# A two-block transformer kernel: norms at four stage borders done by token halves

## The reference, cut to what matters

```python
def _rms(t, g):
    y = t * lax.rsqrt(jnp.mean(t * t, axis=-1, keepdims=True) + NORM_EPS)
    return y * g
def _modulate(t, g, shift, scale):
    return _rms(t, g) * (1 + scale) + shift
def _swiglu(h, w13, w2):
    gte, up = jnp.split(h @ w13, 2, axis=-1)
    return (jax.nn.silu(gte) * up) @ w2
...
lat = lat + 0.5 * mod[:, 0, 2] * _swiglu(_modulate(lat, norm_g[i, 0], mod[:, 0, 0], mod[:, 0, 1]), ffn_w13[i, 0], ffn_w2[i, 0])
h = _modulate(lat, norm_g[i, 1], mod[:, 1, 0], mod[:, 1, 1])
...
lat = lat + mod[:, 1, 2] * y
```

## Time and profile before

| | |
|---|---|
| median of three runs | 2087.09 us |
| profiled execution | 2086.57 us, span 2084.8 us |
| mean granted TensorE clock | 0.961 |
| PE busy | 1910.5 us (92%) |
| DVE busy | 1403.1 us (67%) |
| ACT busy | 683.8 us (33%) |
| POOL busy | 123.0 us (6%) |
| DMA | 315.79 MB, 151 GB/s over the span |

### The profile page before, as it was taken

How to read it: one execution, slowest core, us unless ns; L and a number is a source line. 1 busy time by engine, 2 the same in 40 slices (tenths; PEclk the granted TensorE clock), 3 DMA queues, 4 the chain that set the end, 5 groups by cost and what they waited for, 6 DMA issues and landing times.

```text
span 2084.8 us, 26715 instructions
## 1 busy us (share of the span) xinstructions
PE 1910.5 (92%) x10092; PEld 1624.6 (78%) x10092; DVE 1403.1 (67%) x2091; ACT 683.8 (33%) x910; POOL 123.0 (6%) x78
## 2 busy tenths in 40 slices
PE   2975799799999998997999999989999998889998
PEld 2954788678888887886888888878888887679998
DVE  7868899876666666668766666776665225856554
ACT  2443356332222223332322222132222123444432
POOL 2000200200000110002000001100000010010000
PEclk9976899899999999998999999999999999999999
DMA  9840955433334443434244334424433323223444
GB/s 377 309 176 26 247 193 198 156 120 141 133 148 148 154 172 121 151 131 159 113 151 149 133 140 168 167 110 151 151 138 115 101 93 120 91 81 141 164 162 158
DMA packets 75738, 315.79 MB, mean 151 GB/s; under 512 B 19060, under 2 KB 22904, under 8 KB 56344
## 3 DMA queue, kind: packets, MB, share of 16 engines
q1 hardware_dynamic: 75136, 314.15, 42.6%
q10 hardware_dynamic: 536, 0.79, 0.1%
HBM read 313.86 MB, written 1.06 MB: 151 GB/s over the span
## 4 chain that ended last, share of the span: by engine, by line
PE 74%; DVE 17%; ACT 3%; issue 2%; DMA 1%; SPq 1%; POOL 0%; DVEq 0%; ACTq 0%
PE acc L1296 72%; DVE Wl L811 4%; ACT Wh L526 2%; DVE tmp L798 2%; PE psN L1296 1%; DVE psGT L843 1%; DVE psGT L846 1%; DVE najunk L846 1%; DVE najunk L843 1%; DMA afirst<-in_ada_w 1%; DVE small L968 1%; DVE XT L798 1%; DVE psGT L840 1%; DVE tmp L986 1%; PE psN L1358 0%
## 5 line engine op out<-in xcount | busy, mean ns | idle before, releaser
L1296 PE MATMUL acc<-Hh,Wh 128*128 128x512 f32 (+1 forms) x2320 | 808.4, 348 | 50.1 <-DVE Hl L798 24.2
L1296 PE MATMUL acc<-Hl,Wh 128*128 128x512 f32 (+1 forms) x2320 | 800.3, 345 | 0.0
L1296 PE MATMUL acc<-Hh,Wl 128*128 128x512 f32 (+1 forms) x2320 | 799.6, 345 | 0.0
L811 DVE TENSOR_TENSOR Wl<-raw,Wh 128x2048 fp32r<-128x2048 f32 (+1 forms) x214 | 449.6, 2101 | 273.4 <-ACT Wh L526 273.3
L1296 PEld LDWEIGHTS acc<-Hh,Wh 128*128 128x128 f32 x2320 | 448.3, 193 | 113.7 <-issue 46.0
L526 ACT ACTIVATE Wh<-raw 128x2048 fp32r<-128x2048 f32 (+1 forms) x214 | 374.3, 1749 | 350.0 <-PE acc L1296 331.8
L1296 PEld LDWEIGHTS acc<-Hl,Wh 128*128 128x128 f32 x2320 | 448.6, 193 | 50.7 <-issue 0.7
L1296 PEld LDWEIGHTS acc<-Hh,Wl 128*128 128x128 f32 x2320 | 447.9, 193 | 50.4
L1296 PE MATMUL acc<-hidh,Wh 128*128 128x512 f32 (+1 forms) x704 | 258.6, 367 | 0.9 <-DVE Wl L811 0.9
L1296 PE MATMUL acc<-hidl,Wh 128*128 128x512 f32 (+1 forms) x704 | 258.3, 367 | 0.0
L1296 PE MATMUL acc<-hidh,Wl 128*128 128x512 f32 (+1 forms) x704 | 258.2, 367 | 0.0
(11 more groups left out here) (222 smaller groups left out, 1189.9 us busy)
## 6 DMA issues: line engine op xcount, KB each, us to landing
raw<-in_ffn_up SPq DMA_DIRECT2D x88, 1024.0 KB, 4.8
graw<-in_mod_w SPq DMA_DIRECT2D x144, 512.0 KB, 5.5
raw<-in_ffn_down SPq DMA_DIRECT2D x64, 704.0 KB, 4.1
graw<-in_ada_w SPq DMA_DIRECT2D x32, 512.0 KB, 6.8
raw<-in_odd_in SPq DMA_DIRECT2D x16, 1024.0 KB, 5.0
raw<-in_even_in SPq DMA_DIRECT2D x12, 1024.0 KB, 7.2
raw<-in_conv_in SPq DMA_DIRECT2D x12, 1024.0 KB, 4.8
afirst<-in_ada_w SPq DMA_DIRECT2D x8, 1024.0 KB, 13.1
```

Source lines behind the costliest of these rows:

```text
L811: nc.vector.tensor_tensor(Wl[:, half, 0:f], raw[:, slot, 0:f], Wh[:, half, 0:f].bitcast(f32), ALU.subtract)\
L1296: return nc.tensor.matmul(out, lhsT, rhs, start=start, stop=stop)
```

## The change

At the four borders into conv_in, ffn1_up, ffn2_up and gqa_kv (`HALVED`) the last tiles, the norm and the first two tiles are done by halves of the tokens. The latent half is CL, the context half CC.

- The last output (the last two down tiles, or the last tile of conv_out) is made for the latent columns first, then for the context columns. The latent residual, squares, sums, mean, root and spread go on beside the context columns of PE. New semaphores `lat_*` order them.
- `halves_norm` on DVE runs the eight latent chunks and then the eight context chunks. The context residual stands behind the third latent chunk, the context mean behind the sixth.
- The split of the first weight tile moves from before the last down tile to between the first latent chunks, in two halves of 1024 columns; the second tile's split is also halved and stands behind the sixth and the eighth latent chunk. (At ffn1_up the first tile is split whole behind the latent mean.)
- On PE the first two tiles run as: tile 0 latent, tile 1 latent, tile 0 context, tile 1 context. In gqa_kv: keys latent, value blocks 0 and 1, keys context, value blocks 2 and 3.
- conv_out makes one modulation row a tile instead of two (its four tiles), gqa_out one instead of none.

The core of the diff:

```diff
-    ("conv_out", 4, 16, 0, TOK, 2, "dve"),
+    ("conv_out", 4, 16, 0, TOK, 1, "dve"),
...
-    ("gqa_out", 4, 16, 0, LAT, 0, "dve"),
+    ("gqa_out", 4, 16, 0, LAT, 1, "dve"),
...
+            def halves_norm(name, meanwhile):
...
+                dve.wait_ge(lat_done, l + 1)
+                residual_half(0, CL).then_inc(lat_res, 1)
+                meanwhile()
+                mean(0, psN, lat_ss, l + 1).then_inc(lat_mean, 1)
+                if not ffn:
+                    split(S[name].n0)
+                dve.wait_ge(lat_spread, l + 1)
+                scaled(0, 0, CL, psN).then_inc(lat_t, 1)
+                for k in range(KC):
+                    if k + 1 < KC:
+                        if k > 0:
+                            dve.wait_ge(lat_ready, KC * l + k)
+                        scaled(k + 1, 0, CL, psN).then_inc(lat_t, 1)
+                    if ffn and k < 2:
+                        split_half(S[name].n0, k)
+                    dve.wait_ge(lat_hi, KC * l + k + 1)
+                    low(k, 0, CL).then_inc(lat_ready, 1)
+                    if k in (5, 7):
+                        split_half(S[name].n0 + 1, k // 2 - 2)
+                    if k == 2:
+                        dve.wait_ge(tile_done, s.n0 + s.tiles)
+                        residual_half(1, CC).then_inc(drained["dve"], 1)
+                    if k == 5:
+                        mean(1, psT[1], n_ss, i + 1).then_inc(n_mean, 1)
...
+                def last_halved():
...
+                    part(0, 0, CL)
+                    sum_of_sums(name)
+                    part(0, 1, CL).then_inc(lat_done, 1)
+                    part(1, 0, CC, lat_sums).then_inc(tile_done, 1)
+                    lat_spreads(name)
+                    part(1, 1, CC).then_inc(tile_done, 1)
...
+                pe.wait_ge(lo_ready, s.n0 + 1)
+                part(0, CL, lat_ready, KC * l, {3: ctx_sums, 7: ctx_spread})
+                pe.wait_ge(lo_ready, s.n0 + 2)
+                pe.wait_ge(drained["dve"], prev.drained1)
+                part(1, CL, lat_ready, KC * l, {})
+                part(0, CC, h_ready, H0[name], {}).then_inc(tile_done, 1)
+                part(1, CC, h_ready, H0[name], {}).then_inc(tile_done, 1)
...
+                if name in HALVED:
+                    n0, ffn = S[name].n0, S[X_FROM[name]].tiles > KC
+                    if ffn:
+                        split_half(n0, 0)
+                    for k in range(KC):
+                        if k == 1 and ffn:
+                            split_half(n0, 1)
+                        if k in (4, 6):
+                            split_half(n0 + 1, k // 2 - 2)
+                        act.wait_ge(lat_t, KC * HALVED[name] + k + 1)
+                        nc.scalar.activation(Hh[:, k, CL], tmp[:, k % 2, CL], ACT.Identity, bias=affine(name, k, 0)[1])\
+                            .then_inc(lat_hi, 1)
+                        if k == 2:
+                            act.wait_ge(drained["dve"], S[X_FROM[name]].drained1)
+                            for q in LAST[name]:
+                                square_half(name, q, CC)
```

More of the change, by code:

```diff
@@ L212, in build @@
         c_tanh = sem("c_tanh")
+        hi_half = sem("hi_half")
+        lat_done, lat_res, lat_sq, lat_ss, lat_mean, lat_rstd, lat_spread, lat_t, lat_hi, lat_ready = (
+            sem("lat_" + x) for x in ("done", "res", "sq", "ss", "mean", "rstd", "spread", "t", "hi", "ready"))
         nmx = small[:, 0:64]
@@ L292, in build, with halved @@
         X_TO = {f: n for n, f in X_FROM.items()}
+        HALVED = {n: i for i, n in enumerate(["conv_in", "ffn1_up", "ffn2_up", "gqa_kv"])}
+        LAST = {n: (KC - 2, KC - 1) if n == "ffn1_up" else (KC - 1,) for n in HALVED}
+        LAT_SQ0 = {n: sum(len(LAST[m]) for m in HALVED if HALVED[m] < HALVED[n]) for n in HALVED}
+        CL, CC = slice(0, LAT), slice(LAT, TOK)
+        def halved(s):
+            return X_TO.get(s.name) in HALVED
         def summed_of(s):
@@ L1304, in three, with first_two_halved, part @@
                 return mm(out, wl, xh, False, last)
+            def first_two_halved(s):
+                name, prev = s.name, S[X_FROM[s.name]]
+                l = HALVED[name]
+                def part(t, c, ready, base, beside):
+                    n = s.n0 + t
+                    for k in range(KC):
+                        pe.wait_ge(ready, base + k + 1)
+                        for j in range(2):
+                            last = three(acc[t][j][:, c], n % SPLIT, j * KC + k, Hh[:, k, c], Hl[:, k, c], k == 0, k == KC - 1)
+                        if k in beside:
+                            beside[k](name)
+                    return last
+                pe.wait_ge(lo_ready, s.n0 + 1)
[5 more added lines that the diff above has]
+                part(1, CC, h_ready, H0[name], {}).then_inc(tile_done, 1)
@@ new lines, in lat_sums, with lat_spreads @@
+            def lat_sums(name):
+                pe.wait_ge(lat_sq, LAT_SQ0[name] + len(LAST[name]))
+                for q in LAST[name]:
+                    for b in range(2):
+                        ins = nc.tensor.matmul(psN[:, b:b + 1], tmp[:, q % 2, b * P:(b + 1) * P], ones[:, 0:1],
+                                               start=False, stop=q == KC - 1, skip_group_check=True)
+                ins.then_inc(lat_ss, 1)
+            def lat_spreads(name):
+                pe.wait_ge(lat_rstd, HALVED[name] + 1)
+                for b in range(2):
+                    ins = spread(psN[:, b * P:(b + 1) * P], rstd, b)
+                ins.then_inc(lat_spread, 1)
@@ new lines, in ctx_sums, with ctx_spread @@
+            def ctx_sums(name):
+                pe.wait_ge(n_sq, KC * NORMS[name] + KC)
+                for q in LAST[name]:
+                    for b in range(2):
+                        ins = nc.tensor.matmul(psT[1][:, b:b + 1], tmp[:, q % 2, (2 + b) * P:(3 + b) * P], ones[:, 0:1],
+                                               start=False, stop=q == KC - 1, skip_group_check=True)
+                ins.then_inc(n_ss, 1)
+            def ctx_spread(name):
+                pe.wait_ge(n_rstd, NORMS[name] + 1)
+                for b in range(2):
+                    ins = spread(psT[1][:, b * P:(b + 1) * P], rstd, 2 + b)
+                ins.then_inc(n_spread, 1)
@@ L1322, in step @@
                     last.then_inc(tile_done, 1)
-                if begin:
+                if begin or halved(s):
                     for t in range(begin, s.tiles):
                         step(t, t % SPLIT, t // SPLIT)
+                elif s.name in HALVED:
+                    first_two_halved(s)
+                    tiles(pe, s, SPLIT, 0, lambda t, u, i: None if isinstance(t, int) and t < SPLIT else step(t, u, i), head=1)
                 else:
@@ L1363, in sum_of_sums @@
                 pe.wait_ge(n_sum, SUM0[name] + SUMMED[name])
+                if name in HALVED:
+                    for h, bank in enumerate((psN, psT[1])):
+                        for b in range(2):
+                            nc.tensor.matmul(bank[:, b:b + 1], tmp[:, 2, (2 * h + b) * P:(2 * h + b + 1) * P], ones[:, 0:1],
+                                             start=b == 0, stop=False, skip_group_check=True)
+                    return
                 sum_of(name, tmp[:, 2, :], True, False)
```

126 lines of the change are left out of this document (116 added, 10 removed).

## The result

The changed kernel took 2077.81 us (median of 5, 2076.37 to 2078.04) against 2087.49 for the kernel before (2086.03 to 2087.95): ratio 0.995, 95% interval 0.9939 to 0.9961. That is 9.7 us less; 13.3 were forecast, and the time is inside the range. The profiled execution took 2077.92, its span is 8.7 shorter. The page of after, beside the earlier trace rows: the span, the engines' busy time, and the shares of the chain of waits.

The account below looks back on a forecast made before the run. PE, busy 92%, was taken as the bound, with time to win only at stage borders. 4.6 + 5.8 + 3.3 + 4.9 - 3.7 = 14.9, less 1.6 for hand-overs, left 13.3: 2073.8 us, range 2067 to 2083.

Parts of the forecast that it names:

- conv_in, 4.6: Border into conv_in: last pair's start to second tile's end falls from 49.5 to 44.9 us, gaining 4.6.
- The walk: Step-by-step PE and DVE schedule of the conv_in border after the change: low parts at 16.3 to 26.3, end 44.9 us.
- ffn1_up, 5.8: Border into ffn1_up: 50.8 us falls to 45.0, with one modulation row fewer and a 1.2 third-tile wait; gain 5.8.
- ffn2_up, 3.3: Border into ffn2_up: same schedule as conv_in, but PE waits 1.2 for the third tile's weights; 49.4 us before, gain 3.3.
- gqa_kv, 4.9: Border into gqa_kv: 52.1 us falls to 46.6, plus 0.6 wait for the key norm; gain 4.9.
- gqa_out, -3.7: Four modulation rows moved into gqa_out delay its residuals and the stop into ffn3_up: cost 3.7 us, bounds 1.8 and 5.5.
- Hand-overs, -1.6: At the four borders, some eight uncharged hand-overs between engines each: 0.4 us a border, 1.6 taken off the gain.
- Rival 1: PE's clock falls to half in the chunk-paced stretches at the borders, losing 6 to 8 us: about 2080.5; chance 0.23.
- signs of being wrong: Listed at the borders: half clock, Wl wait over 3 us, low parts 1.6 apart, PE waiting for latent sums inside down tiles.
- Rival 2: The modulation rows moved to gqa_out cost nothing net there: 2070 us; chance 0.11.
- Rival 3: At the borders the chunk chain does not overlap, 1.6 us a chunk instead of 0.91: about 2093.5; chance 0.09.
- Rival 4: Third tiles wait for weights, each border giving back 3 us: about 2086; chance 0.05.

Follow-up runs that it names:

- E4: Changed kernel with the third tile's weights of ffn1_up and ffn2_up split in two halves by output block: 2075.23 us.
- E6: Changed kernel with ffn2_down's sixteen modulation rows (none in odd_out, conv_out, gqa_q, gqa_out), halved third-tile weights, ffn1_up's early low split and in-block transposes: 2059.07 us.
- E10: The same kernel as E6, run again: 2059.13 us.
- E1: Kernel before with only the moved modulation rows (conv_out one a tile, gqa_out one), no norm by halves: 2087.4 us.
- E7: Changed kernel with only the border into ffn1_up put back to whole 512-token norm and tiles: 2075.96 us.
- E2: Changed kernel with the modulation rows put back (conv_out two a tile, gqa_out none), so halves only: 2079.69 us.
- E3: Changed kernel with one modulation row a tile in ffn2_down and none in odd_out, conv_out, gqa_q and gqa_out: 2065.78 us.
- E8: E3 with the border into ffn1_up put back to whole 512-token norm and first two tiles: 2066.41 us.
- E9: Changed kernel with DVE's low split of ffn1_up's first weights moved ahead of the latent mean: 2076.87 us.

## Why the prediction was right, and where its terms were not

- **conv_in, 4.6:** measured 4.56, and the same in nine kernels with that half norm. The walk held to 0.8 us at every low part.
- **ffn1_up, 5.8:** measured 4.64 and 4.85. Mis-sized by three pieces, each seen: the first Hh matmul 16.45 us after the last tile's start (960.33 to 976.78) instead of 15.8; the third tile's stop worth 1.3 to 1.5 (E4), not 1.2; half clock for 3.4 us, worth 0.5 (E6 against E10, which differ there by it). These are 1.3 to 1.5 where 1.0 to 1.2 are missing. And the reason was wrong, which the sum hid: the walk counts one row less (2.7, as the expectations of E1 and E7 price it) and leaves 3.1 to the halves. E1 and E7 show that the row gives all of it (4.0 to 5.65, less half clock included) and the halves 0 within 1; without the row they cost 1.6 (E2), and with no row in that stage at all they bring 0.5 (E3 against E8). What they save in the stop is given back: PE has no down tile behind the transposes (1.73 against conv_in's 0.39), waits 0.59 for a sum, 1.39 for weights, and runs 3.4 us at half clock.
- **ffn2_up, 3.3:** 2.90; E4 gives 1.61 for the third tile's stop where I took 1.2 (and 6.84 - 5.76 is only 1.1). With 1.61 my own walk gives 2.9.
- **gqa_kv, 4.9:** 4.99, against the one trace of before. Against E1, whose stop has the same code and less half clock, it is 4.1; so the closeness is in part luck.
- **gqa_out, -3.7:** -3.95, of which the rows are 3.34 to 3.4 (E1; after less E2), and 0.57 stands in the stop into ffn3_up, where it goes with the half clock of the first tile (E6 and E10, above) and not with the rows. In the last three tiles the first product of a row took 1.75 to 1.77 us and the second 1.24 to 1.59, between my 1.23 and 2.33. Each of the five long ones had started while POOL was in a sum, and ended 1.09 to 1.10 after the end of that sum (1844.24 + 2.23 = 1846.47, and 1845.80 + 1.77 = 1847.57); so did the four of 2.14 to 2.33 in conv_out's last two tiles before, 1.08 to 1.10 after. The sums here are of 256 columns and had less left when the product came, which is why 1.77 and not 2.33. By the Trainium skill (SBUF — State Buffer, section SBUF: two separate sides) a VectorE operation with two SBUF inputs and a GpSimd operation shut each other out for a whole instruction. The trace agrees: POOL's power took 2.69 against 0.71 (E9), and each of these products ended about 1.1 us after POOL's sum, as if it had begun there.
- **Hand-overs, -1.6:** not there. The walks of conv_in and gqa_kv came out within 0.1 without them; the allowance happened to cover what ffn1_up and ffn2_up fell short. That was luck.
- **Sum.** The places of the prediction gave 17.1 - 3.95 = 13.1 of the 13.3, so close because misses of either sign cancelled. The rest of the way to 8.7 is outside it: 2.8 of half clock in the attention and gqa_out's first tile, 1.4 at the start, 0.4 in ffn3. E1 shows the half clock in the attention without halves, E6 and E10 show that in gqa_out's first tile present and absent in one kernel, and the start differs by up to 3 us between kernels with the same start. The kernel before has neither stretch in its one profiled execution, which was also 0.9 under its median; by medians the gain is 9.7. Whether half clock in the attention is as frequent before as after stays open: there is only one trace of before.

**Rivals.** Rival 1 (clock in the paced stretch) came true at one border of four, for 0.5 us and not 1.5 to 2. At that border, ffn1_up, two of the signs of being wrong stood: this half clock, and PE waiting 0.59 for a sum inside the last tile; together they cost about 1.1 us. Rival 2: no, E1 prices gqa_out at 3.34. Rival 3: at conv_in three of the seven steps between low parts were 0.66 to 0.91, the four with a split or a residual between them, on DVE or ACT, 1.35 to 2.05, 1.4 on average as in the walk. Rival 4: the stops are 1.36 and 1.39, half of the 3 it needed. The Trainium skill's rule that the throttled state is the default after idleness (TensorE: Matmul & The Clock Gate, Part 1), taken literally, gave no fall at these borders; the trace shows one, behind single gaps of 1.73 and 1.49 us, so the measurement decides against that reading.
